# RWKV features: three stages and a copy folded into one, running sums as mask products, Sigmoid as Tanh, GpSimd left out, and the features laid in memory tile by tile

## What is computed

```python
kk = to_heads(k * k_k, RWKV_HEADS)
kk = kk * lax.rsqrt(jnp.sum(kk * kk, axis=-1, keepdims=True) + 1e-12)
for d, (dw, da) in enumerate(((dw_f, da_f), (dw_b, da_b))):
    w_log = -softplus(-(w0[d] + tanh(dw) @ w_up[d])) - 0.5
    decay = exp(-exp(w_log))
    a = sigmoid(a0[d] + da @ a_up[d])
    k_d = k * (1 + (a - 1) * k_a)
    dirs.append((decay, k_d, kk * a))
# the scan then works on them; the readout needs r * 0.5 * (k_d forward + k_d backward) * r_k
```

## Time and profile before

| | us |
|---|---|
| median of three runs | 3813.18 (3811.79 to 3821.56) |
| profiled execution, its own time | 3820.33 |
| its span | 3818.7 |
| TensorE matmul, busy | 3082.6 (81%) |
| VectorE, busy | 1664.8 (44%) |
| ScalarE, busy | 1102.3 (29%) |
| GpSimd, busy | 172.3 (5%) |
| mean granted TensorE clock | 0.872 |

### The profile page before, as it was taken

How to read it: one execution, slowest core, us unless ns; L and a number is a source line. 1 busy time by engine, 2 the same in 40 slices (tenths; PEclk the granted TensorE clock), 3 DMA queues, 4 the chain that set the end, 5 groups by cost and what they waited for, 6 DMA issues and landing times. The chain is left out here.

```text
span 3818.7 us, 53162 instructions
## 1 busy us (share of the span) xinstructions
PE 3082.6 (81%) x22408; PEld 2360.9 (62%) x22408; DVE 1664.8 (44%) x2774; ACT 1102.3 (29%) x1988; POOL 172.3 (5%) x192
## 2 busy tenths in 40 slices
PE   7599688798735888558799998698658699799998
PEld 2488256577514787324688787356347477678876
DVE  5411446344464334446444323355364333535432
ACT  5311267222142322211322122462311232232222
POOL 0000000000052111010000000000011000000000
PEclk9799699899866999658899998779768799889999
DMA  8221100033022111010223232202100122223321
GB/s 298 65 64 53 20 1 18 28 90 109 7 85 86 36 36 36 30 55 0 77 83 94 86 91 58 90 1 61 29 1 1 56 78 89 66 61 90 99 83 66
DMA packets 231966, 236.59 MB, mean 62 GB/s; under 512 B 27696, under 2 KB 205104, under 8 KB 231665
## 3 DMA queue, kind: packets, MB, share of 16 engines
q1 hardware_dynamic: 231426, 232.02, 19.9%
q10 hardware_dynamic: 304, 1.18, 0.1%
HBM read 213.55 MB, written 19.09 MB: 61 GB/s over the span
## 5 line engine op out<-in xcount | busy, mean ns | idle before, releaser
L189 DVE TENSOR_TENSOR second_w_low<-second_w_raw,second_w_high 128x1024 fp32r<-128x1024 f32 (+1 forms) x228 | 271.3, 1197 | 528.7 <-ACT second_w_high L185 528.5
L185 ACT CAST second_w_high<-second_w_raw 128x1024 fp32r<-128x1024 f32 (+1 forms) x228 | 232.0, 1023 | 723.2 <-PE ffn_in_acc L210 249.8
L208 PE MATMUL ffn_in_acc<-ffn_h_high,second_w_high 128*128 128x512 f32 x704 | 282.7, 402 | 16.3 <-DVE ffn_h_low L459 16.3
L210 PE MATMUL ffn_in_acc<-ffn_h_high,second_w_low 128*128 128x512 f32 x704 | 284.6, 404 | 0.0
L209 PE MATMUL ffn_in_acc<-ffn_h_low,second_w_high 128*128 128x512 f32 x704 | 281.3, 400 | 0.0
L189 DVE TENSOR_TENSOR first_w_low<-first_w_raw,first_w_high 128x1024 fp32r<-128x1024 f32 x115 | 139.6, 1223 | 257.1 <-ACT first_w_high L185 255.9
L185 ACT CAST first_w_high<-first_w_raw 128x1024 fp32r<-128x1024 f32 x115 | 119.5, 1048 | 270.8 <-PE attn_in_acc L210 100.7
L208 PEld LDWEIGHTS ffn_in_acc<-ffn_h_high,second_w_high 128*128 128x128 f32 x704 | 134.5, 191 | 50.7 <-issue 19.7
L209 PEld LDWEIGHTS ffn_in_acc<-ffn_h_low,second_w_high 128*128 128x128 f32 x704 | 134.6, 191 | 34.3 <-issue 0.5
L210 PEld LDWEIGHTS ffn_in_acc<-ffn_h_high,second_w_low 128*128 128x128 f32 x704 | 134.5, 191 | 31.2
L208 PE MATMUL ffn_down_acc<-ffn_mid_high,second_w_high 128*128 128x512 f32 x352 | 142.5, 405 | 11.8 <-DVE second_w_low L189 11.8
(11 more groups left out here) (754 smaller groups left out, 6890.6 us busy)
## 6 DMA issues: line engine op xcount, KB each, us to landing
second_w_raw<-in_ffn_w_gate SPq DMA_DIRECT2D x44, 512.0 KB, 3.8
second_w_raw<-in_ffn_w_up SPq DMA_DIRECT2D x44, 512.0 KB, 3.8
second_w_raw<-in_ffn_w_down SPq DMA_DIRECT2D x40, 512.0 KB, 3.4
first_w_raw<-in_rec_w_in SPq DMA_DIRECT2D x33, 512.0 KB, 3.9
first_w_raw<-in_attn_ada_w SPq DMA_DIRECT2D x24, 512.0 KB, 4.8
first_w_raw<-in_rec_ada_w SPq DMA_DIRECT2D x24, 512.0 KB, 4.7
s_feat<-rwkv_feat_out SPq DMA_DIRECT2D x32, 384.0 KB, 3.1
rwkv_feat<-s_feat SPq DMA_DIRECT2D x48, 256.0 KB, 4.1
```

Of the source, the lines that this page charges most:

```text
L185: act.copy(self.view(self.high[b % self.splits], b), self.view(self.raw[b % self.bufs], b)).then_inc(self.high_done, 1)
L189: dve.tensor_tensor(self.view(self.low[b % self.splits], b), self.view(self.raw[b % self.bufs], b), self.view(self.high[b % self.splits], ...
L208: pe.matmul(out, sh, mh, start=(first and j == 0), stop=False)
L210: ins = pe.matmul(out, sl, mh, start=False, stop=(last and j == len(parts) - 1))
```

## The change

- The stages `rwkv_vt`, `rwkv_v` and `rwkv_kk` are gone as stages; their work is part of `rwkv_features`, spread over its engines. ScalarE takes the copies of v that VectorE made.
- The square sums of k are taken token by token: the squares are the stationary operand and a mask of two columns moves, so that 768 tokens by 8 heads lie as 128 by 48. Root and reciprocal run on that; six transposes turn it back to 8 rows.
- The decay gate is computed with tokens on the partitions, 12 gates of 128 tokens by 512 channels: ones times the diagonal of w0 adds the bias, then a product with 32 rows. ScalarE takes Tanh of half of it. Tanh stands for Sigmoid in both gates (sigmoid(x) = 0.5 + 0.5 tanh(x/2)).
- The running sums, both of them, come from products of this gate with a mask `c_sums` of 65 columns a chunk, and a product with ones for the constant part. One Exp makes `decay` (65 columns a chunk, of which "before" and "up to" are two views), a second `growth`.
- The rate gate is a product with 32 rows.
- GpSimd does nothing. k_d and the bonus go to ScalarE (Identity, copy) and VectorE.
- Ten tiles of features; the first of them lie in `y` and `ctx`. Rates and keys have three buffers, the other two features two.
- `s_feat` becomes [direction, tile, channel, feature, block, token]. A store is written in six pieces of 128 tokens per partition; a scan group is loaded by one DMA of 8 KB per partition.
- The semaphores of the stage: 29 instead of 14 (and 13 in the three stages that go).

The core of the diff (the new `rwkv_features`, without its semaphore list):

```diff
+        up, sums, pick = st.sb("up", [P, 512]), st.sb("sums", [P, 2, 3 * 2 * CUM]), st.sb("pick", [8, 4 * P])
+        tiles = [s[:, TT * i:TT * i + TT] for s in spare for i in range(s.shape[1] // TT)]
+        tiles += [st.sb(f"tile{i}", [P, TT])[:] for i in range(10 - len(tiles))]
...
         @block.sync
         def _(sp):
...
+            for n in range(n_units):
                 sp.wait_ge(features, n + 1)
+                for j, (tile, sem) in enumerate(((out[n % 2][0], saved_out[n % 2]), (out[n % 2][1], saved_out[n % 2]),
+                                                 (rates[n % 3], saved_keys[n % 3]), (keys[n % 3], saved_keys[n % 3]))):
+                    sp.dma_start(d["s_feat"][n // 4, :, :, j, n % 4, :].rearrange("c p t -> p c t"),
+                                 tile.rearrange("p (c t) -> p c t", t=P)).then_inc(sem, 16)
...
         @block.tensor
         def _(pe):
+            def gate(g):
+                dr, t, to = g // nt, g % nt, gate_ps[:, (g % 2) * BANK:(g % 2 + 1) * BANK]
+                if g >= 2:
+                    pe.wait_ge(gate_done, g - 1)
+                pe.matmul(to, c["ones"], w0[:, dr].rearrange("p i f -> p (i f)"), start=True, stop=False)
+                r = slice(32 * dr, 32 * dr + 32)
+                pe.matmul(to, lora[r, t * P:(t + 1) * P], up[r, :], start=False, stop=True).then_inc(gated, 1)
+
+            def unit(n):
...
+                for t0, tn in spans(TT, BANK):
+                    ins = pe.matmul(pair_ps[:, t0:t0 + tn], up[r, i * P:(i + 1) * P], lora[r, t0:t0 + tn],
+                                    start=True, stop=True)
+                ins.then_inc(rate_gated, 1)
+                if n >= 2:
+                    pe.wait_ge(exps, n - 1)
...
+                pe.wait_ge(gate_done, nt * (dr + 1))
+                for b in range(2):
+                    for t in range(3):
+                        at = b * BANK + t * 2 * CUM
+                        pe.matmul(unit_ps[n % 2][:, at:at + 2 * CUM], log_w[dr][:, 3 * b + t, i * P:(i + 1) * P],
+                                  sums[:, dr, 0:2 * CUM], start=(t == 0), stop=False, skip_group_check=True)
+                    ins = pe.matmul(unit_ps[n % 2][:, b * BANK:b * BANK + 6 * CUM], c["ones"], sums[:, dr, :],
+                                    start=False, stop=True, skip_group_check=True)
+                ins.then_inc(logs, 1)
...
+            for g in range(2):
+                gate(g)
+            for i in range(4):
+                pe.wait_ge(squared, i + 1)
+                for t in range(nt):
+                    ins = pe.matmul(pair_ps[:, t * 8 + 2 * i:t * 8 + 2 * i + 2], (rates, keys)[i // 2][i % 2][:, t * P:(t + 1) * P],
+                                    c["pick_sum64"][:, 16:18], start=True, stop=True)
+            ins.then_inc(summed, 1)
+            for g in range(2, 4):
+                gate(g)
...
+            for g in range(4, nt):
+                gate(g)
+            for n in range(n_units):
+                unit(n)
+                if n < 3:
+                    for g in (nt + 2 * n, nt + 2 * n + 1):
+                        gate(g)
...
         @block.scalar
         def _(act):
...
+            def rates_of(n):
+                dr, i = n // 4, n % 4
+                act.wait_ge(rate_gated, n + 1)
...
+                act.activation(rates[n % 3], pair_ps[:, 0:TT], ACT.Tanh, scale=0.5,
+                               bias=half_a0[:, 4 * dr + i:4 * dr + i + 1]).then_inc(rate_done, 1)
+                act.wait_ge(rate_done, n + 1)
+                act.activation(keys[n % 3], rates[n % 3], ACT.Identity, scale=half_ka[:, i:i + 1],
+                               bias=not_ka[:, i:i + 1]).then_inc(key_scale, 1)
...
+            act.activation(lora[0:64, :], lora[0:64, :], ACT.Tanh).then_inc(tanhed, 1)
+            for i in range(4):
+                act.activation((rates, keys)[i // 2][i % 2], us[:, 4 + i, :], ACT.Square,
+                               scale=v("rwkv_k_k", i, 1)).then_inc(squared, 1)
+                turned_v(i)
...
+            for n in range(n_units):
+                exponentials(n)
+                if n + 1 < n_units:
+                    rates_of(n + 1)
+                if n < 3:
+                    for g in (nt + 2 * n, nt + 2 * n + 1):
+                        gate(g)
+                if n < 4:
+                    act.wait_ge(keyed, n + 1)
+                    act.copy(bonus[:, n, :], keys[n % 3][:, 0:S]).then_inc(kept, 1)
...
         @block.vector
         def _(dve):
...
+            for n in range(n_units):
...
+                dve.wait_ge(key_scale, n + 1)
+                rated = mine.mark(dve.scalar_tensor_tensor(out=rates[n % 3], in0=rates[n % 3], scalar=1.0, in1=kk[:, i, :],
+                                                           op0=ALU.add, op1=ALU.mult))
+                dve.tensor_tensor(keys[n % 3], keys[n % 3], us[:, 4 + i, :], ALU.mult).then_inc(keyed, 1)
+                if n >= 2:
+                    dve.wait_ge(saved_out[n % 2], 32 * (n // 2))
+                dve.wait_ge(exps, n + 1)
+                dve.tensor_tensor(chunked(o[0]), chunked(kk[:, i, :]), before, ALU.mult)
+                dve.tensor_tensor(chunked(o[1]), chunked(us[:, i, :]), upto, ALU.mult)
+                dve.tensor_copy(ends[:, dr, i, :], arr[:, :, 0 if dr else CH])
...
+                if dr == 0:
+                    dve.wait_ge(kept, n + 1)
                 else:
+                    added = mine.mark(dve.tensor_tensor(bonus[:, i, :], bonus[:, i, :], keys[n % 3][:, 0:S], ALU.add))
...
+                dve.tensor_tensor(keys[n % 3], keys[n % 3], grow[:], ALU.mult).then_inc(features, 1)
...
@@ rwkv_scan
-                for j in range(4):
-                    sp.dma_start(feats[dr][:, j], d["s_feat"][dr, j].rearrange("(i p) t -> p i t", p=P)
-                                 [:, :, tile * P:tile * P + P]).then_inc(landed[dr], 16)
+                sp.dma_start(feats[dr][:], d["s_feat"][dr, tile]).then_inc(landed[dr], 16)
```

More of the change, by code:

```diff
@@ L1275, with __init__, mark, wait @@
 PADDED = TT + 4
[L1278 to L1299 removed]
+class Own:
+    def __init__(self, engine, sem):
+        self.engine, self.sem, self.n = engine, sem, 0
+    def mark(self, ins):
+        self.n += 1
+        ins.then_inc(self.sem, 1)
+        return self.n
+    def wait(self, n):
+        self.engine.wait_ge(self.sem, n)
@@ new lines, in _ @@
+            for t in range(nt):
+                at = BANK + t * P if t < 4 else (t - 2) * P
+                ins = pe.transpose(pair_ps[0:8, at:at + P], rk[:, t * 8:t * 8 + 8], c["ident"])
+            ins.then_inc(turned, 1)
+            pe.wait_ge(rows_kept, 2)
+            pe.wait_ge(v_stored, nt)
+            for i in range(4):
+                if i >= 2:
+                    pe.wait_ge(normed, i - 1)
+                for t0, tn in spans(TT, BANK):
+                    ins = pe.matmul(unit_ps[i % 2][:, t0:t0 + tn], pick[:, i * P:(i + 1) * P], rk_rows[:, t0:t0 + tn],
+                                    start=True, stop=True)
+                ins.then_inc(spread, 1)
@@ L1402, in _ @@
[L1402 to L1418 removed]
+            mine = Own(dve, own)
```

235 lines of the change are left out of this document (116 added, 119 removed).

## The result

The changed kernel takes 3790.64 us (median of 4 runs, 3783.35 to 3795.49) against 3817.37 for the kernel before in the same measurement: ratio 0.9929 [0.9904, 0.9954], 27 us less. Forecast were 3763.0 and a range of 3742 to 3790. The direction is right, the size is half of the forecast. In a later measurement the changed kernel took 3783.71 against 3816.78, 33 us less. Two profiled executions, 3820.33 us before and 3783.35 after (the fastest of its four), differ by 37.0, and their spans by 37.1.

The account below looks back on a forecast made before the run. The prediction saw a chain handing over between engines, none filling the 173.2 us stretch. Its terms summed to 123.0 us, a gain of 50.2 against the median of 3813.18: 3763.0 us, range 3742 to 3790.

Parts of the forecast that it names:

- A gain of 50.2: From the first transpose of the stage to the first scan matmul: 123.0 us instead of 173.2.
- the head of the stage: From the first transpose to the first finished features (unit 0): forecast to be done at 58.2 us.
- units 1 and 2: Second and third of the stage's eight feature units: TensorE does rate gate, mask products and two gates, 9 us each.
- spreads: Four eight-row TensorE products in the stage's head, after the roots are turned: 10.3 us at the slow clock.
- The clock model: TensorE in the stage: slow for first gates, spreads and up to unit 0; fast for square sums, gates 2 and 3, mostly later.
- Tables: ScalarE in the stage: one table load at the start, one for the root, one back; none between Tanh and Exp.
- The VectorE price: In the stage, a 768-column VectorE product costs 0.87 us in a row, 0.95 between two starts, with GpSimd idle.
- the walk through ScalarE's queue: Unit 0's last product waits for the bonus copy, queued behind the next unit's Tanh and Identity and two gate Tanhs.
- (a): Rival on the granted clock in the stage's head: fast throughout; inside the range of 3742 to 3790; chance 0.15.
- (b): Rival: slow clock throughout, TensorE the bound everywhere; stage 154.6 us, gain 18.6, median 3795; chance 0.12.
- The scan itself, and all behind it: Sign to check: the scan and everything after it stay unchanged within 2 us.
- of all groups only the first was waited for: Scan loads: the later loads are worth nothing, since only the first group's load had been waited for.

Follow-up runs that it names:

- padded: Features with old layout, late output sums and filler matmuls in TensorE's waits, plus the stage's short matmuls zero-filled to 128 rows: 3726.24 us, 0.9755.
- with and without pause: Changed kernel with a stage of VectorE clears (3 or 7 x 512 columns) before the scan: 3770.97 or 3779.00 us; without, measured again: 3783.71.
- shifted program: Changed kernel with 284 useless TensorE matmuls added, 190 at the feature stage's end and 94 at the scan's door: 3782.05 us.
- paced kernel: Changed kernel, layout kept, each scan load from the third group on split into four 256 KB transfers issued one after another: 3779.25 us, 0.9898.
- shifted kernels: Useless TensorE matmuls added ahead of the scan: 91 in the kernel before, 3841.33 us; 284 in the changed kernel, 3782.05 us.
- kernel with the features only: Changed kernel with the old layout of `s_feat`, so four stores a unit and four loads a scan group as before: 3777.39 us, 0.9893.

## Why the prediction was half right

*Stage: right in sum, by terms that cancel.* "A gain of 50.2" was 48.9. That it came so close is in part luck: the head of the stage was 3.6 us longer than forecast (61.8 instead of 58.2), units 1 and 2 were 3.4 shorter. Within it:

| step | forecast | measured |
|---|---|---|
| transposes | 5.9 | 5.1 |
| gates 0, 1 | 6.9, slow | 4.1, fast |
| square sums | 5.1, fast | 7.9, slow but for their start |
| gates 2, 3 | 3.4, fast | 8.0, slow |
| turning the roots | 2.1 | 2.4 |
| spreads | 10.3, slow | 10.5 |
| gates 4, 5, unit 0's rate gate and mask products | 14.8, slow | 14.3, slow |
| from there to features 0 | 9.7 | 9.5 |
| units 1, 2 | 9 each | 7.3 each, fast |
| unit 3, units 4 to 7 | 5.4, 6.9 each | 5.3, 6.8 each |
| last product to scan's first issue | 7.0 + 1.1 | 8.7 |
| first load to first turn | 5.7 | 6.7 |

The clock model had the levels right for the spreads, for what follows them up to unit 0, and for the late units. It had them wrong in the first gates, half of whose matmuls have 32 rows and which ran fast, and in the square sums and the two gates behind them: I had called the sums full height and therefore fast. They are full height and two columns wide. The terms were priced by records of 512 columns at 0.86 us slow and 0.43 fast: that held for the spreads (10.60 at 0.50 and, padded, 5.59 at 1.00, against 10.3 and 5.2), but a gate, priced at 3.4 or 1.7, took 4.0 at 0.50 and 2.05 at 1.00. The price of the square sums held as well, 25 records in 5.00 us at 0.50.

Tables: that Tanh and Sigmoid take a load each, 1.28 us, is in these lines of the kernel before (L1366 is the Tanh, the load of L1372 is for Sigmoid):

```profile
1046.89 1.28 ACT L1366 ACT_TABLE_LOAD   x1 [18.23 <-PEq L38]
1048.18 0.84 ACT L1366 ACTIVATE rec_shifted<-rec_shifted 64x768 f32<-64x768 f32 x1
1049.05 1.28 ACT L1372 ACT_TABLE_LOAD   x1
```

That none would stand between Tanh and Exp was an assumption when it was made. It held: behind the load at 1037.30 the changed stage has none, while Tanh (L1433, L1447) and Exp (L1459, L1461) alternate through eight units.

The VectorE price (0.95 a product, no 2 us with GpSimd idle) and the order of hand-overs held; the first bonus copy released L1537 after 3.95 us of idle, as the walk through ScalarE's queue had it. The rivals fall with these rows: the head was neither fast throughout, for which (a) stands in the chances (0.15) and in the range, nor slow throughout (b), there were two table loads in the stage (the first Tanh needed none), the stores ran at 282 GB/s against the 294 taken and hid up to the last unit, and VectorE was fast. The load took a microsecond more than forecast, as I had counted one load of 1 MB at 390 GB/s and two were in flight at 300.

*Scan: the step that failed.* "The scan itself, and all behind it, unchanged within 2 us: if that moves more, the sum is wrong in a part that it does not treat." It moved by 15.3, and by 11.5 to 13.0 in the other executions of the changed kernel, with and without pause: a term put at nothing for no better reason than equal code. I had looked for what the change does to the scan's data (first load, waits for later loads), found nothing, and took equal code for equal time. Two things that the code shares with what runs ahead of it were left out. The first is the place of TensorE's instructions among the pieces in which, as I read it, they arrive; by that reading it makes the 5.2 us of idle time, by stalls and the wait for `inv` behind them. The second is the granted clock, which falls 5 times in this scan even in the kernel before: 14 falls instead make the 10.1 us of busy time, and what makes them more is open. The expected row "of all groups only the first was waited for" was right, and yet the loads cost: not by being late, but by stalls (issue 7.0 us with the later loads, 1.0 without them). The numbers close, though not by the scan alone: 3817.37 in this measurement, less the 50.2 of the sum, less 2.2 that the rest gave beyond it (37.1 + 15.3 - 50.2), plus 15.3 for the scan, plus 10.3 since the profiled execution of the kernel before lay 3.0 over its median and that of after 7.3 under: 3790.6. The last term is the spread of single executions and no property of the change; measured again, the same kernel took 3783.71, inside the range, so that it is chance on which side of 3790 a measurement falls. The 15.3 of the scan is not. With the scan at 333.0, as in the shifted program, and all else as measured, the median would be 3775.6 by this sum, an estimate.

*Open.* What sets the number of falls in a kernel, and with it two thirds of the scan's loss, is not settled: the paced kernel has one short stall (0.5 us) and 12 falls. Shown is that they all but vanish when TensorE's waits are filled (0 or 1 left), and that their number is another in the shifted kernels and in the one without the later loads. Why the layout adds stalls (idle 56.6 instead of 52.5) was not separated into one transfer against four.

## What to carry to other kernels

A stage whose engines hand over at fine grain was here not independent of what ran ahead of it (332.7 and 348.0 us with the same code): check its length for itself, not the total alone, when another part is changed, and allow some per cent of it (here 4.6) as the uncertainty of such a forecast. Where stalls marked issue go with loads in flight (here 7.0 us with them, 1.0 without), look at them by source line and see what else is late then; an operation that nobody needs soon (here the output sums, 14.3 us of scan) belongs behind the one that the next engine waits for. And try short matmuls at full height with zeros where they run back to back (the spreads took 5.59 us instead of 10.60), and matmuls of no use in TensorE's regular waits if, and only if, the wait covers them (groups of 27.5 us where it did, 28.8 where it did not).

## What the runs showed of the hardware

- The granted clock fell from 1.00 to 0.50 while TensorE was busy without a gap, in the 48 products of 128 rows and two columns (1.00 up to 1021, 0.50 from 1022 to 1027 with 5.00 us busy), and stayed there through 32-row and 8-row products (0.50 from 1027 to 1035 and from 1037.3 to 1047.9). With the 32-row and 8-row products padded to 128 rows it still fell in the square sums (mean 0.67), but was back at 1.00 before the spreads and held through them and the gates behind them (1.00 from 1040 to 1056).
- A 1 MB load with pieces of 8 KB reached 434 GB/s in a slice. But from the scan's first issue to its first turn, with two loads in flight, the new layout bought little: 6.7 us against 7.1 in the kernel with the features only, and 5.8 against 6.75 behind the old stage.
- Stores in pieces of 512 bytes ran at 282 GB/s with the DMA engines busy for 0.99 of the time, those in rows of 3072 bytes at 390 with 0.97.
- Pieces of 16 KB arrived on the instruction queue, one about every 5 us of the changed kernel's scan (66 in 348 us), and all seven stalls of TensorE that are marked issue ended 1.2 to 1.6 us after one of them. With a load of 1 MB in flight TensorE stood still for up to 1.6 us (1.9 when measured again); without the later loads for 0.7 at most, with loads in paced quarters for 0.5.
- In the scan of the kernel with the features only, the second group, with a fall of the granted clock, took 29.1 us and the third, without one, 27.5.
